# Head scans of a gated DeltaNet layer: the value convolution's later taps as whole-row multiply and add on GpSimd instead of thirds of a row on VectorE

## The reference

```python
def dwconv_centred(x, w, b):
    n = x.shape[1]
    xp = jnp.pad(x, ((0, 0), (CONV_PAD_L, CONV_K - 1 - CONV_PAD_L), (0, 0)))
    y = xp[:, 0:n] * w[0]
    for i in range(1, CONV_K):
        y = y + xp[:, i:i + n] * w[i]
    return y + b
...
    qkv = jax.nn.silu(dwconv_centred(qkv, p['conv_a_w'], p['conv_a_b']))
    q, k, v = jnp.split(qkv, [D_QK, 2 * D_QK], axis=-1)
```

## Time and profile before

| | |
|---|---|
| median of three runs | 1491.56 us |
| the three runs | 1488.91 to 1491.62 us |
| span of the profiled execution, first to last instruction | 1486.6 us |
| PE busy | 1470.7 us |
| DVE busy | 1016.3 us |
| ACT busy | 798.8 us |
| POOL busy | 350.0 us |

### The profile page before, as it was taken

One profiled execution on the slowest core, in us unless ns is written; L12 is line 12 of the kernel. 1 busy time (PEld: TensorE's weight loads), 2 busy tenths in 40 slices (PEclk: granted clock), 3 DMA queues, 4 the chain that ended last, 5 costly groups with the idle time before them and its releaser, 6 DMA issues.

```text
span 1486.6 us, 28072 instructions
## 1 busy us (share of the span) xinstructions
PE 1470.7 (99%) x11376; PEld 1414.7 (95%) x11376; DVE 1016.3 (68%) x1815; ACT 798.8 (54%) x1645; POOL 350.0 (24%) x296
## 2 busy tenths in 40 slices
PE   9999999999999999999999999999999999999997
PEld 8899999999999999999899999999999999999886
DVE  5789897988889898888847744744836711544254
ACT  6574857566584857566476564574576500322111
POOL 3122322232232322132211221221221211342110
PEclk9999999999999999999999999999999999999999
DMA  9322121122213112222311221211212531543132
GB/s 322 112 69 90 33 74 54 45 80 63 79 33 110 30 52 81 88 79 89 114 51 46 82 62 49 82 55 56 82 52 90 170 123 43 169 145 105 43 127 99
DMA packets 122435, 127.46 MB, mean 86 GB/s; under 512 B 6745, under 2 KB 105922, under 8 KB 122306
## 3 DMA queue, kind: packets, MB, share of 16 engines
q1 hardware_dynamic: 122018, 125.34, 26.6%
q10 hardware_dynamic: 288, 0.33, 0.1%
HBM read 105.56 MB, written 20.09 MB: 85 GB/s over the span
## 4 chain that ended last, share of the span: by engine, by line
PE 95%; DVE 2%; SPq 1%; DMA 1%; issue 1%; ACT 0%; POOLq 0%; POOL 0%; DVEq 0%
PE mb L136 16%; PE mb L135 16%; PE mb L134 16%; PE db L134 10%; PE db L136 9%; PE db L135 9%; PE db L1374 2%; PE db L1346 2%; PE db L1390 2%; PE db L1363 2%; PE db L1384 2%; PE db L1008 2%; PE db L1315 1%; PE db L1233 1%; PE db L1194 1%; PE db L1298 1%
## 5 line engine op out<-in xcount | busy, mean ns | idle before, releaser
L134 PE MATMUL mb<-h_hi,w_hi 128*128 128x384 f32 x1080 | 363.0, 336 | 0.0
L135 PE MATMUL mb<-h_lo,w_hi 128*128 128x384 f32 x1080 | 362.9, 336 | 0.0
L136 PE MATMUL mb<-h_hi,w_lo 128*128 128x384 f32 x1080 | 362.9, 336 | 0.0
L134 PE MATMUL db<-h_hi,w_hi 128*128 128x384 f32 x816 | 287.9, 353 | 0.2 <-DVE w_lo L1472 0.2
L136 PE MATMUL db<-h_hi,w_lo 128*128 128x384 f32 x816 | 274.6, 336 | 0.0
L135 PE MATMUL db<-h_lo,w_hi 128*128 128x384 f32 x816 | 274.5, 336 | 0.0
L2074 POOL TENSOR_TENSOR w_lo<-w,w_hi 128x1024 fp32r<-128x1024 f32 x47 | 127.3, 2709 | 459.4 <-ACT w_hi L2109 459.4
L134 PEld LDWEIGHTS mb<-h_hi,w_hi 128*128 128x128 f32 x1080 | 203.0, 188 | 0.1
L136 PEld LDWEIGHTS mb<-h_hi,w_lo 128*128 128x128 f32 x1080 | 203.0, 188 | 0.0
L135 PEld LDWEIGHTS mb<-h_lo,w_hi 128*128 128x128 f32 x1080 | 203.0, 188 | 0.0
L134 PEld LDWEIGHTS db<-h_hi,w_hi 128*128 128x128 f32 x816 | 153.7, 188 | 4.1 <-DVE w_lo L1472 0.7
(11 more groups left out here) (339 smaller groups left out, 2909.4 us busy)
## 6 DMA issues: line engine op xcount, KB each, us to landing
w<-in_w_in SPq DMA_DIRECT2D x48, 512.0 KB, 4.0
d_dt<-decay_rows SPq DMA_DIRECT2D x16, 576.0 KB, 6.7
d_qg<-decay_rows SPq DMA_DIRECT2D x16, 512.0 KB, 4.1
w<-in_w_gate SPq DMA_DIRECT2D x16, 512.0 KB, 4.1
branch_a<-d_kq SPq DMA_DIRECT2D x8, 576.0 KB, 3.3
branch_b<-l_z SPq DMA_DIRECT2D x8, 576.0 KB, 2.8
merge_gates_b<-l_gates SPq DMA_DIRECT2D x8, 576.0 KB, 5.5
m_in<-merge_gates_b SPq DMA_DIRECT2D x8, 576.0 KB
```

Source lines behind the costliest of these rows:

```text
L134: pe.matmul(out, hi, rhi, start=(k == 0), stop=False)
L135: pe.matmul(out, hi, rlo, start=False, stop=False)
L136: return pe.matmul(out, lo, rhi, start=False, stop=(last and stop))
```

## The change

Taps 1 to 3 of the next value leave DVE, and each becomes two instructions on POOL, whole rows long: the shifted row times its weight into the scratch row `cb_`, then `v2` plus `cb_`. Tap 1 stands right behind the nine block copies and ahead of `select_decays`; taps 2 and 3 stand behind `clear_tail`. ACT takes the SiLU of the value in one operation at the end of step 7. The semaphore `taps` no longer counts the value from head 1 on; `vtap` counts two for each tap.

```diff
@@ front_gpsimd
+            def value_tap(h, a):
+                par = R.par[:, PA_CONV + (a * 3 + QKV[1]) * H + h:PA_CONV + (a * 3 + QKV[1]) * H + h + 1]
+                if a == 1:
+                    pool.wait_ge(S["tap0"], 3 * (h - 1) + 2)
+                else:
+                    pool.wait_ge(S["vtap"], value_done(h - 1) + 2 * (a - 1))
+                if a == 1:
+                    pool.wait_ge(S["ssq_mm"], h)
+                pool.tensor_scalar(cb_[:, :], row_of(h - 1, 1)[:, a:a + CONV], par, None, ALU.mult).then_inc(S["vtap"], 1)
+                pool.wait_ge(S["vtap"], value_done(h - 1) + 2 * a - 1)
+                pool.tensor_tensor(v2[:, :], v2[:, :], cb_[:, :], ALU.add).then_inc(S["vtap"], 1)
...
                 if not last:
+                    pool.wait_ge(S["w1p"], (h + 1) * 5)
+                    pool.wait_ge(S["w2p"], (h + 1) * 4)
+                    value_tap(h + 1, 1)
                     select_decays(h + 1)
                     pool.wait_ge(S["w1d"], (h + 1) * 2)
                     clear_tail(h + 1)
+                    for a in range(2, TAPS):
+                        value_tap(h + 1, a)
                     low(block_of(h + 1, 0))
@@ front_scalar, scan steps
                         elif s == 7:
-                            silu_value(h + 1, 0)
-                            silu_value(h + 1, 1)
-                        elif s == 8:
-                            silu_value(h + 1, 2)
+                            silu(h + 1, 1)
@@ front_vector, scan steps
-                    if not last:
-                        pieces = [(a, part) for a in range(1, TAPS) for part in range(NTHIRD)]
-                        for a, part in (pieces[0:2] if s == 0 else pieces[s + 1:s + 2]):
-                            value_tap(h + 1, a, part)
```

More of the change, by code:

```diff
@@ L251, in front_stage @@
         PIECES = tuple((a, at, min(at + 386, CONV)) for a in (2, 3) for at in range(0, CONV, 386))
-        THIRDS = (0, 386, 772, CONV)
-        NTHIRD = len(THIRDS) - 1
         vinv = lambda d, t: (w1, w2)[d][:, d * NT + t, :]
@@ L294, in front_stage @@
         order = lambda h, s: 3 * h + ((0, 2, 1)[s] if h == 0 else s)
+        taps_done = lambda h, s: (1, 3, 2)[s] if h == 0 else 2 * h + (2, 0, 3)[s]
+        value_done = lambda h: 2 * (TAPS - 1) * h
         QKV = (1, 2, 0)
@@ L436, in third_in @@
                 if k == 3:
-                    sp.wait_ge(S["taps"], 3 * H)
+                    sp.wait_ge(S["taps"], taps_done(H - 1, 2))
                 elif k == 4:
@@ L633, in next_key @@
                 if g == 0:
-                    act.wait_ge(S["taps"], order(h, 1) + 1)
+                    if h:
+                        act.wait_ge(S["vtap"], value_done(h))
+                    else:
+                        act.wait_ge(S["taps"], taps_done(0, 1))
                 if h == H - 1:
@@ L641, in next_value @@
                 if g == 0:
-                    act.wait_ge(S["taps"], 3 * h + 3)
+                    act.wait_ge(S["taps"], taps_done(h, 2) if h else taps_done(0, 1))
                 if h == H - 1:
@@ L657, in z_out @@
                     if h < H - 1:
-                        act.wait_ge(S["taps"], 3 * h + 4)
+                        act.wait_ge(S["taps"], taps_done(h + 1, 0))
                     else:
@@ L676, in silu @@
             def silu(h, s):
-                act.wait_ge(S["taps"], order(h, s) + 1)
+                if h and s == 1:
+                    act.wait_ge(S["vtap"], value_done(h))
+                else:
+                    act.wait_ge(S["taps"], taps_done(h, s))
                 dst = (k2[:, h % 2, :], v2[:, :], q2[:, :])[s]
                 act.activation(dst, dst, ACT.Silu).then_inc(S["silu"], 1)
[L681 to L689, removed]
             def square_q(h):
@@ L1423, in conv @@
                         ins.then_inc(S["taps"], 1)
[L1425 to L1434, removed]
             def lru_tap(a):
```

## The result

The changed kernel takes 1532.6 us (median of 4 runs, 1531.9 to 1533.54) against 1490.24 for the kernel before (4 runs, 1488.76 to 1491.62): 1.0285 of its time, 95% interval 1.027 to 1.0299. So it is 42.4 us slower. The prediction said slower, 1515, with a range up to 1526; the time lies outside it.

A forecast was written before the change was run, and what follows sets the result against it. PE, busy 99% of the span, was taken as the bound, held up by DVE at each scan's start. 21.0 + 4 - 2.9 + 1.7 = 23.8 us on 1491.56 gave 1515, range 1505 to 1526.

The forecast's parts named there:

- L1766 late: Ahead of the scan, DVE's copy that PE awaits starts 3.1 us late in six heads, 2.4 in head 2: 21.0 us.
- Rival (c): Tap 1's multiply on POOL is near two-input length, costing every head 1.5 us more: 1526 us; chance 0.07.
- The selection meets `scaled_query(0)`: At the scan's start, POOL's selection holds DVE's `scaled_query(0)` by 0 to 1.2 us a head, 0.6 taken: +4 us.
- The pieces leave the scan: Scan steps without DVE's tap pieces get shorter, and heads 0 and 4 regain step 0 losses: together -2.9 us.
- Taps 2 and 3 hidden: In the scan behind the selection, POOL's taps 2 and 3 take 7.6 us and cost 0.
- One SiLU: At the end of step 7, ACT's single SiLU delays `vn` of step 8, 0.25 us a head: +1.7 us.
- Rival (a): Ahead of the scan DVE keeps its turn and POOL waits; only `scaled_query(0)` is held: 9 us, 1501; chance 0.07.
- Rival (b): POOL's multiply and add don't block DVE ahead of the scan: 1486 to 1490 us, not slower; chance 0.06.

The follow-up runs named there:

- E1: The changed kernel with tap 1 moved on POOL from ahead of the selection to behind the clearing, next to taps 2 and 3: 1487.99 us, ratio 0.9987.
- E2: The changed kernel with the taps' multiply on POOL by a constant 0.5 instead of the column of weights: 1532.11 us, ratio 1.0278.
- E7: As E1, with the taps' multiplies replaced by an unshifted multiply, a copy and a product of two tensors: 1487.57 us, a single run.
- E4: The changed kernel with 36 identity matmuls on PE ahead of the wait for L1766's copy, heads 0 to 6: 1526.83 us, ratio 1.0256.
- E8: The changed kernel with tap 1's multiply over only 396 of its 1155 elements: 1511.99 us, ratio 1.0159.
- E3: The changed kernel without taps 1 to 3 of the value from head 1 on, on any engine: 1488.4 us, ratio 0.9987.

## Why the prediction was wrong

The direction and the mechanism hold: DVE and POOL take turns ahead of the scan, L1766 is late, PE waits, and the other terms come out near their numbers. Two terms carry the miss. In order of the sum:

- **L1766 late: predicted 21.0, measured 33.2.** The failed step is "Its length no row shows ... I take 1.1 us". The multiply is 3.23 us (E1), not 1.1, and above the stated upper bound of 2.75. Both the value and the bound came from rows of other operations, the affine_select and the two-input add, as if one input couldn't be slower than two. E1 shows that it can, 3.23 us beside 2.66, and E2 and E7 that neither the column nor the shift is the reason. A smaller error is that the key tap ends 0.96 us after the multiply instead of 1.24. The add is right: it ends 2.48 us after the key tap (230.80 to 233.28), where 2.53 was forecast. Rival (c), "the multiply is slow", was the right branch, with 0.07 for it. Its 1.5 us more a head is near the 1.7 measured (12.2 over seven heads); its 1526 lacks the clock.
- **The clock: not in the prediction, measured +6.3** (E4 against after; after against before has +5.5 in that column, since the -0.8 of the pieces in step 0 stands in it too). I forecast a gap of 3 us on PE and put no price on what comes after it. Even at my own multiply this was worth 3.7 (E8).
- **The selection meets `scaled_query(0)`: predicted +4, measured +5.4.** The number is inside the bounds, at 0.77 a head, but the picture behind it isn't that of the forecast. I expected both orders among the seven heads, for L1767's end and the selection's arrival to be nearly at one time. L1766 came so late that the selection was ahead in every head, each time with the same 0.77 us. In E8, where the two do come together, a head loses 0 to 1.03 us and the seven 1.8. That the mean taken fits is luck.
- **The pieces leave the scan: predicted -2.9, measured -2.1 in the steps and -0.8 in step 0 (E1).** Right, by the step period too: 2.87 against 2.91.
- **Taps 2 and 3 hidden: predicted 0, measured 0** (E1 against E3). They take 2 x (3.23 + 2.66) = 11.8 us and not 7.6, for the same mis-sized multiply, and the cover reaches that far.
- **One SiLU: predicted +1.7, measured +1.4.** Right.

The sum of these is 33.2 + 6.3 + 5.4 - 2.9 + 1.4 = 43.4 where 23.8 was forecast, so 19.6 more: 12.2 the multiply, 6.3 the clock, 1.4 the collision, -0.3 SiLU. The medians are 17.2 apart (1532.6 and 1515.4): the forecast was added to 1491.56, and the kernel before has a median of 1490.24 here, while the time of after stands 1.9 above its span and not the 5.0 that I had added. So 3.1 us of the miss are hidden by the base of the sum. What the prediction would have said with the right length, 1515.4 + 12.2 = 1527.6, still lacks the clock.

Rival (a), that DVE keeps its turn, falls with the timeline of after: the multiply went between two key taps that stood back to back. Rival (b), that nothing is blocked, falls with 3.64 us for 1.22.

## What to carry to other kernels

Price an operation on the engine that will run it, from a run of that form: that one input takes less than two was assumed here, and the length was wrong by a factor of nearly three. Before work is moved into an engine's idle time, ask what the neighbour reads meanwhile: POOL's reads were free beside DVE's scan operations, which have an operand in PSUM, and hidden beside the query taps behind the scan, which PE doesn't wait for. They cost 44 us, the clock with them, beside its key taps, at the one place where DVE has 0.27 us of slack. And a gap that you add on PE can have a second price, the slower clock behind it (0.9 us a head here), which wants its own line in the sum.

## What was not expected of the hardware

- POOL's TENSOR_SCALAR multiply of 128x1155 takes 3.23 us, with the scalar a column or a constant, the row shifted or not. Its copy takes 1.15, the product with the weight as a broadcast tensor 2.11, the sum of two tensors 2.66. DVE does a TENSOR_SCALAR of the same shape, with a multiply and an add in it, in 1.12 us (L1441 of the kernel before). The Trainium skill, page "GPSIMD Engine Reference", section 4.1, has one-input operations at roughly line rate and two-input ones about twice as slow as VectorE. The copy fits; the multiply does not, and the measurement decides.
- A gap of 4.8 us on PE is followed by 3.4 or 6.8 us at half clock, in all seven heads; one of 2.5 us by 3.4 us in four of seven (E8); with the identity matmuls in it, by none (E4). In E2, with the same gaps, it is the other way round, 3.4 us in heads 0, 2, 4 and 6 and 6.8 in 1, 3 and 5, so it isn't a property of the head. Why it is the one length or the other wasn't tried.
- DVE's key tap ends sooner after the multiply than its own length of 1.42 us: 0.96 us in after and 0.51 in E8. `scaled_query(1)`, 1.22 us alone, ends 1.08 after the add. So a part of POOL's recorded instruction doesn't block, 0.46 and 0.91 us of the two multiplies and 0.14 of the add. What part, stays open.
